# Attention gate rows by one product with ones per 512 columns, in place of columns, diagonals and a spread

## What is computed

```python
cond = jax.nn.silu(c)
mod = cond @ mod_w[i] + mod_b[i]
sh_m, sc_m, gt_m, sh_f, sc_f, gt_f = jnp.split(mod[:, None, :], 6, axis=-1)
h = rms_norm(x, norm_g[i, 0]) * (1.0 + sc_m) + sh_m
y = swa_sink_attention(h, w_qkv[j], w_o[j], swa_sinks[j], cos, sin)
x = x + gt_m * rms_norm(y, norm_g[i, 1])
h = rms_norm(x, norm_g[i, 2]) * (1.0 + sc_f) + sh_f
x = x + gt_f * rms_norm(swiglu(h, ffn_w_in[i], ffn_w_out[i]), norm_g[i, 3])
```

## Time and profile before

| | us |
|---|---|
| median of 3 runs | 1093.65 (1093.56 to 1093.86) |
| profiled execution | 1093.3 |
| its span on the engines | 1091.5 |
| PE busy | 1057.7 (97%) |
| DVE busy | 688.9 (63%) |
| ACT busy | 488.8 (45%) |
| POOL busy | 23.4 (2%) |

### The profile page before, as it was taken

One profiled execution on the slowest core, in us unless ns is written; L12 is line 12 of the kernel. 1 busy time (PEld: TensorE's weight loads), 2 busy tenths in 40 slices (PEclk: granted clock), 3 DMA queues, 4 the chain that ended last, 5 costly groups with the idle time before them and its releaser, 6 DMA issues.

```text
span 1091.5 us, 13612 instructions
## 1 busy us (share of the span) xinstructions
PE 1057.7 (97%) x4976; PEld 837.1 (77%) x4976; DVE 688.9 (63%) x877; ACT 488.8 (45%) x623; POOL 23.4 (2%) x34
## 2 busy tenths in 40 slices
PE   5899999999999999999999999999999999999998
PEld 2566676667678878888888888888888888888885
DVE  3778796787889795767667545444444544444445
ACT  4433475767466334434333333343344444444444
POOL 0000000000011000000000000000000000000000
PEclk9899999999999999999999999999999999999999
DMA  9999989999984895777678555555554555555542
GB/s 360 418 417 416 414 343 355 361 410 370 370 321 165 293 355 193 308 270 299 252 272 313 214 189 190 192 192 192 192 183 164 189 193 196 192 192 192 192 154 77
DMA packets 50599, 288.23 MB, mean 264 GB/s; under 512 B 6401, under 2 KB 6401, under 8 KB 23937
## 3 DMA queue, kind: packets, MB, share of 16 engines
q1 hardware_dynamic: 47090, 268.47, 65.2%
q0 software_dynamic: 2304, 16.78, 3.8%
q10 hardware_dynamic: 1168, 2.49, 0.7%
HBM read 285.36 MB, written 2.10 MB: 263 GB/s over the span
## 4 chain that ended last, share of the span: by engine, by line
PE 78%; DMA 10%; DVE 5%; ACT 4%; issue 2%; SPq 0%; POOL 0%; ACTq 0%; DVEq 0%
PE ps L1452 25%; PE ps L1454 24%; PE ps L1453 24%; DMA raw<-in_w_qkv 5%; DMA mraw<-in_mod_w 3%; ACT whi L428 2%; DVE wlo L848 2%; PE ps L1476 2%; DMA graw<-in_mod_h 2%; DVE mraw L859 1%; PE ps L1516 1%; PE ps L1636 1%; ACT pS L529 1%; PE ps L1727 1%; ACT pS L517 0%
## 5 line engine op out<-in xcount | busy, mean ns | idle before, releaser
L848 DVE TENSOR_TENSOR wlo<-raw,whi 128x1024 fp32r<-128x1024 f32 x334 | 394.3, 1221 | 305.2 <-ACT whi L428 305.2
L428 ACT ACTIVATE whi<-raw 128x2048 fp32r<-128x2048 f32 x167 | 320.1, 1917 | 411.0 <-PE ps L1454 377.4
L1452 PE MATMUL ps<-whi,hThi 128*128 128x512 f32 x1224 | 482.4, 394 | 10.0 <-DVE hTlo L905 7.6
L1454 PE MATMUL ps<-whi,hTlo 128*128 128x512 f32 x1224 | 477.4, 390 | 0.0
L1453 PE MATMUL ps<-wlo,hThi 128*128 128x512 f32 x1224 | 477.2, 390 | 0.0
L1452 PEld LDWEIGHTS ps<-whi,hThi 128*128 128x128 f32 x1224 | 230.3, 188 | 77.0 <-issue 20.9
L1454 PEld LDWEIGHTS ps<-whi,hTlo 128*128 128x128 f32 x1224 | 230.2, 188 | 48.5
L1453 PEld LDWEIGHTS ps<-wlo,hThi 128*128 128x128 f32 x1224 | 230.5, 188 | 46.5
L859 DVE CUSTOM_DVE_ANT_0 mraw<-mraw,cb,mbias 128x1024 f32<-128x1024 f32 x64 | 80.6, 1279 | 24.3 <-DMA mraw<-in_mod_w 24.0
L859 DVE CUSTOM_DVE_ANT_0 mraw<-mraw,cb,modT 128x1024 f32<-128x1024 f32 x64 | 83.0, 1308 | 13.3 <-DMA mraw<-in_mod_w 13.1
L1452 PE MATMUL ps<-whi,oThi 128*128 128x512 f32 x112 | 45.5, 406 | 0.3 <-DVE wlo L848 0.3
(11 more groups left out here) (192 smaller groups left out, 553.5 us busy)
## 6 DMA issues: line engine op xcount, KB each, us to landing
raw<-in_w_in SPq DMA_DIRECT2D x88, 1024.0 KB, 4.8
mraw<-in_mod_w SPq DMA_DIRECT2D x128, 512.0 KB, 7.4
raw<-in_w_out SPq DMA_DIRECT2D x44, 1024.0 KB, 4.8
raw<-in_w_qkv SPq DMA_DIRECT2D x24, 1024.0 KB, 14.6
graw<-in_mod_h SPq DMA_DIRECT2D x16, 1024.0 KB, 17.4
raw<-in_w_o SPq DMA_DIRECT2D x16, 1024.0 KB, 6.7
graw<-in_mod_h POOLq DMA_DIRECT2D x12, 1024.0 KB, 8.5
x<-in_x ACTq DMA_DIRECT2D x2, 1024.0 KB, 8.5
```

The source lines that it names most:

```text
L428: A(split_of(q, s)[0], raw[:, s], ACT.Copy).then_inc(hi_done, 1)
L848: V.tensor_tensor(low[:, k], raw[:, s, k], high[:, k].bitcast(F32), ALU.subtract).then_inc(done, 1)
L1452: mm(dst, hi, high[:, n], start=start, stop=False)
L1454: return mm(dst, lo, high[:, n], start=False, stop=stop)
```

## The change

The bias of 512 gate values is written by a small transfer into row 1 of the evacuated sums (`gate_bias`, issued by ACT), where the sums are zero. One product of a 128x128 matrix of ones with the 128x512 sums then gives all 512 gate values with their bias on all partitions at once (`gate_rows`). DVE multiplies the bank by the norm's weight, which a transfer of 1 MB, issued by POOL, has put into `grow` on all partitions beforehand, and writes `grow` (`gate_row`). `columns` for n = 4 to 7, `gate_mod`, the first `vcol`, the two attention `diagonals`, the two attention `spread`s and their `grow_evac`s are gone. The four gate sums 28 to 31 stand together; `sums_out(7)` moves ahead of `hi_of(32)`. The path of the last gate keeps its form, with other counts.

```diff
+        gacc3 = at("gacc3", 42, [P, N])
-        diag1 = at("diag1", 72, [P, 8, P])
...
+        def gate_acc(n):
+            return (gacc2[:, 0], gacc2[:, 1], gacc3[:, :], gacc2[:, 0])[n - 4]
...
 ACT        def sums_out(n):
                 act.wait_ge(g_step, GP * (n + 1))
+                if n >= 4:
+                    if n == 6:
+                        act.wait_ge(rope_c, 5)
+                    if n == 7:
+                        act.wait_ge(rows_pe, 1)
+                    A(gate_acc(n), ps[:, (6, 7, 6, 5)[n - 4]], ACT.Copy).then_inc(g_evac, 1)
+                    return
...
+            def gate_bias(n):
+                act.wait_ge(g_evac, n + 1)
+                act.dma_start(gate_acc(n)[1:2, :], gbias[n - 4:n - 3, :]).then_inc(bias_in[n - 4], 16)
...
             sums_out(4)
             evac_q(2, 1)
+            gate_bias(4)
             hi_of(21)
...
             sums_out(5)
             hi_of(24)
+            gate_bias(5)
...
             sums_out(6)
+            gate_bias(6)
...            (copy_y)
+                    if w:
+                        act.wait_ge(rows_pe, 2 + w)
...
             hi_of(31)
+            sums_out(7)
             hi_of(32)
+            gate_bias(7)
             hi_of(33)
-            sums_out(7)
...
             copy_y(1, 6)
-            grow_evac(0, 4, 0)
             hi_of(35)
...
             square_y(1)
-            grow_evac(1, 6, 0)
...
 DVE
-            def gate_mod(c):
...
+            def gate_row(n):
+                cols = slice((n - 4) * N, (n - 3) * N)
+                dve.wait_ge(rows_pe, n - 3)
+                dve.wait_ge(rows_in, 16)
+                V.tensor_tensor(grow[:, cols], ps[:, ROW_BANKS[n - 4]], grow[:, cols], ALU.mult).then_inc(rows_done, 1)
...
             mods(67, 2)
+            gate_row(4)
             lo_of(32)
             mods(69, 2)
+            gate_row(5)
             lo_of(33)
             mods(71, 2)
+            gate_row(6)
             lo_of(34)
-            gate_mod(3)
-            dve.wait_ge(oT_ready, 8)
-            dve.wait_ge(mod_added, 8)
-            V.tensor_tensor(vcol[:, :], modT[:, 2 * KT:3 * KT], gcol[:, 1], ALU.mult).then_inc(vc, 1)
+            gate_row(7)
             mods(73, 2)
...
 POOL
-            pool.wait_ge(vc, 1)
-            diagonals(diag1, 0)
-            pool.wait_ge(diag_pe, 2)
-            diagonals(diag1, 1)
+            pool.wait_ge(pv_pe, 8)
+            pool.dma_start(grow[:, :], grows).then_inc(rows_in, 16)
...
 PE
+            def gate_rows(n):
+                pe.wait_ge(bias_in[n - 4], 16)
+                if n == 4:
+                    pe.wait_ge(oT_ready, 8)
+                elif n == 6:
+                    pe.wait_ge(g_evac, 8)
+                elif n == 5:
+                    pe.wait_ge(rows_done, 1)
+                else:
+                    pe.wait_ge(rows_done, 2)
+                mm(ps[:, ROW_BANKS[n - 4]], ones[:, :], gate_acc(n), start=True, stop=True).then_inc(rows_pe, 1)
...
-            columns(4)
...
-            columns(5)
...
-            columns(6)
...
             o_block(30)
-            gate_sums(28)
-            gate_sums(29)
+            for p in range(28, 32):
+                gate_sums(p)
+            gate_rows(4)
             o_block(31)
-            gate_sums(30)
-            gate_sums(31)
+            gate_rows(5)
...
             o_block(32)
-            columns(7, 5)
+            gate_rows(6)
             o_block(33)
-            spread(diag1, 0, 4, 0)
+            gate_rows(7)
             o_block(34)
-            pe.wait_ge(half_evac, 14)
-            spread(diag1, 1, 6, 0)
             o_block(35)
...
+ROW_BANKS = (4, 4, 5, 4)
```

More of the change, by code:

```diff
@@ L61, in after, with build @@
     return q + (s + n) // 4, (s + n) % 4
-def build(nc, x, crow, cT, mod_h, pos, invf, mod_w, modbT, gT, w_qkv, w_o, sinks, w_in, w_out, out):
+def build(nc, x, crow, cT, mod_h, pos, invf, mod_w, modbT, gbias, gT, grows, w_qkv, w_o, sinks, w_in, w_out, out):
     with ExitStack() as ctx:
@@ L200, in build @@
         pv_pe, oThi_done, oT_ready = sem("pv_pe"), sem("oThi_done"), sem("oT_ready")
+        bias_in = [sem(f"bias_in{s}") for s in range(4)]
+        rows_in, rows_pe, rows_done = sem("rows_in"), sem("rows_pe"), sem("rows_done")
         vc, diag_done, diag_pe, grow_done = sem("vc"), sem("diag_done"), sem("diag_pe"), sem("grow_done")
@@ L454, in sums_out @@
                 act.wait_ge(g_step, GP * (n + 1))
+                if n >= 4:
[5 more added lines that the diff above has]
+                    return
                 if n >= 2:
                     act.wait_ge(reduced, n - 1)
-                sums = gacc if n < 4 else gacc2
-                A(sums[:, n % 2], ps[:, 6 + n % 2 if n < 7 else 5], ACT.Copy).then_inc(g_evac, 1)
+                A(gacc[:, n % 2], ps[:, 6 + n % 2], ACT.Copy).then_inc(g_evac, 1)
+            def gate_bias(n):
+                act.wait_ge(g_evac, n + 1)
+                act.dma_start(gate_acc(n)[1:2, :], gbias[n - 4:n - 3, :]).then_inc(bias_in[n - 4], 16)
             for b in range(HB):
@@ L775, in f1 @@
                         if tail and u == 1 and s in (0, 2):
-                            grow_evac(s // 2, 4, 4)
+                            grow_evac(s // 2, 4)
             def gk(i, s):
@@ L1124, in gate @@
             def gate(cols, count):
-                dve.wait_ge(grow_done, count)
+                dve.wait_ge(rows_done, count)
                 V.tensor_tensor(y[:, :, cols], y[:, :, cols],
@@ L1197, in _ @@
             dve.wait_ge(ysq, 6)
-            gate(slice(2 * N, 3 * N), 4)
+            gate(slice(2 * N, 3 * N), 3)
             V.tensor_reduce(stat[:, 12:14], ssq[:, :, 0:3], AX.X, ALU.add).then_inc(ychain, 1)
@@ L1489, in sums, with columns @@
                     last.then_inc(g_step, 1)
-            def columns(n, bank=None):
+            def columns(n):
                 pe.wait_ge(g_evac, n + 1)
-                if bank is None:
-                    bank = 6 + n % 2
-                acc = gacc if n < 4 else gacc2
                 for f in range(4):
-                    last = mm(ps[:, bank, f:f + 1], acc[:, n % 2, f * P:(f + 1) * P], ones[:, 0:1],
+                    last = mm(ps[:, 6 + n % 2, f:f + 1], gacc[:, n % 2, f * P:(f + 1) * P], ones[:, 0:1],
                               start=True, stop=True)
                 last.then_inc(reduced, 1)
+            def gate_rows(n):
[9 more added lines that the diff above has]
+                mm(ps[:, ROW_BANKS[n - 4]], ones[:, :], gate_acc(n), start=True, stop=True).then_inc(rows_pe, 1)
             def gate_sums(p):
@@ L1758, in _ @@
             o_block(37, (1,), (2, 1), tiles=(0,))
-            pe.wait_ge(grow_done, 4)
+            pe.wait_ge(rows_done, 4)
             pe.wait_ge(half_evac, 16)
@@ L1799, in f1 @@
                     if tail and s == 0:
-                        spread(diag3, 0, 4, 4)
+                        spread(diag3, 0, 4)
                     if tail and s == 2:
-                        pe.wait_ge(grow_done, 6)
-                        spread(diag3, 1, 4, 4)
+                        pe.wait_ge(grow_done, 2)
+                        spread(diag3, 1, 4)
             with pe.Fori(2, FB - 1) as i:
@@ L1914 @@
         "modbT": cols(inputs["mod_b"][0]),
+        "gbias": np.ascontiguousarray(np.asarray(inputs["mod_b"])[0][2 * D:3 * D].reshape(4, N)),
         "gT": np.ascontiguousarray(gains),
+        "grows": np.ascontiguousarray(np.broadcast_to(np.asarray(inputs["norm_g"])[0, 1], (P, D))),
         "w_qkv": blocks(w_qkv),
```

29 lines of the change are left out of this document (11 added, 18 removed).

## The result

The changed kernel takes 1095.51 us (median of 22 executions, 1093.35 to 1099.64), the kernel before, run beside it, 1093.66 us (22 executions, 1092.34 to 1094.91). The ratio is 1.0019, 95% interval 1.0013 to 1.0025. Forecast were 1093.4 us and no change: the kernel became slower by 1.9 us. The profiled execution took 1096.84 us, its span is 1095.0, 3.5 us over that of before.

A forecast was written before the change was run, and what follows sets the result against it. PE was taken as the bound, with DVE almost level at block 38, where PE's gain becomes a wait; lo_of(35) starting 0.2 us earlier reaches the end: 1093.65 - 0.2 = 1093.4 us, range 1091.0 to 1095.9.

The forecast's parts named there:

- main step: DVE waits at gate_row(7) for PE; lo_of(35) starts at 310.6, 0.2 us earlier; PE waits 2.8 us at block 38.
- Rival (a): At block 38: DVE does not hold it and PE's gain is kept, -2.7 us, 1091.0 us; chance 10%.
- its own bounds, -0.6 and -1.0: Lower bounds on the forecast time: -0.6 us for the bias issue on ACT, -1.0 us for the cover of the columns.
- inner range: Whole kernel: the forecast's own range from its bounds, 1092.0 to 1094.9 us.
- The main sum: Whole kernel: -0.2 us against the median of 1093.65, so 1093.4 us; chance 69%.
- rival (c): PE's wait of 2.8 us ahead of block 38 lowers the clock to 1.2 GHz: 1096.8 us; chance 6%.
- a clock under 1.0 after 325 us: Sign that the forecast is wrong: granted clock below full after 325 us, pointing to rival (c).
- The bias issue: ACT's queue near 193 us, ahead of hi_of(21): one DMA issue adds 0.6 us, bounds 0 and 1.3.
- PE at 283 us: PE's position at 283 us against the kernel before: +0.6 - 0.8 = -0.2 us.
- the sum has 0.8 + 1.8 + 1.7 + 1.27 - 3.4: PE after 283 us: columns(7), two spreads and an idle gap removed, four products of 3.40 us added.
- Rival (b): Late transfers on DVE's chain, deciding from a landing over 8.2 us: +1 to +2.5, 1094.6 to 1096.1 us; chance 15%.
- the 291 that would have counted: grows landing later than about 291 us would stop lo_of(32) and then PE, one for one; 284 to 288 forecast.
- Rival (d): Last gate's diagonals stay, only their counts change; nothing in the tail moves; no own case or chance.

The follow-up runs named there:

- the changed kernel's repeat: The changed kernel unchanged, run again beside the kernel before on another chip: 1094.75 us, ratio 1.0013.
- the filled kernel: Three extra products of 512 columns, results unused, on PE ahead of block 38, against the changed kernel: 1093.56 us, ratio 1.0000 to the kernel before.
- the mended one: mods(73, 2) run ahead of gate_row(7) on DVE, against the changed kernel: 1094.59 us, ratio 1.0019 to the kernel before.

## Why the prediction was wrong

**What it had right.** The chain of its main step stands in the trace. Forecast: DVE waits some 3 us at `gate_row(7)` for PE (2.94 measured), PE arrives early at block 38 and waits 2.8 us (2.90; 2.64 to 2.93 in the five other profiles with this wait), nothing is left at the first spread's place, PE's gain does not arrive. `lo_of(35)` was forecast for 310.6: 311.48 in the profile with the fall at 230 us, 309.66 in one without. And where the clock holds, the time is near the forecast one: 1092.8 to 1093.5 us in the five fastest executions of the changed kernel's repeat, before beside it 1093.18. Part of that closeness is chance. With the wait filled block 38 starts at 325.65, 1.6 us earlier than in before where 0.2 was forecast; 0.8 of that is lost near 465 us, where only that profile has a wait of PE for DVE, and 0.5 behind the last activation (both below). Rival (a), the gain kept, is refuted for this order; its size nearly came once two things behind it were mended, 2.2 us of its 2.7. A slip of addition: with its own bounds, -0.6 and -1.0, the forecast's inner range starts at 1091.8, not 1092.0.

**The step that failed.** The main sum takes the 2.8 us at block 38 only as the place where PE's gain goes; it has no term for the clock behind them, and "0.2 us reaches the end" rests on that. The clock stands only in rival (c), "It decides only if PE's wait at block 38 is longer than any wait that this trace shows to leave the clock full", and its 6%. Its condition was fulfilled by the forecast itself: 2.8 us was the main case's own number, between a row of 1.72 us with full clock and one of 4.19 us with the fall. "2.8 us of waiting is in neither row" was right, and nothing in the two rows makes 6% of it rather than one half. "PE is dense up to the wait" was no protection: before the waits that follow PE is dense too. In the profiles of all kernels here ten waits of 2.17 to 2.93 us stand behind 190 us, and in six the clock fell at the wait or within 1.5 us behind it; behind those of up to 1.6 us it never did. Length alone does not decide: the three at 230 us (2.17, 2.47, 2.69) were all followed by a fall, of the seven at block 38 (2.50 to 2.93) three were; why, no run here shows. The Trainium skill, TensorE: Matmul & The Clock Gate, section HAM oscillation, tells of a kernel whose waits for transfers between bursts of matmuls throttle the clock again each time; these runs show it for single waits of 2.2 to 2.9 us in dense work, though not each time.

The price was too high and the frequency too low. A fall behind block 38 cost 1.5 us (3.4 us at half speed, two profiles) or 2.7 us (6.8 us, one profile), where (c) took 3.4, from the longer one of the earlier trace rows, as the only size. The mean clock of the 22 executions is .9944; the kernel before has .9962 to .9964 on the three chips of the experiments (beside these 22 its clock is not on record). 0.0019 · 1093 = 2.1 us, or 1.2 falls of 1.7 us in an execution as a mean, an estimate: some have none, most have one, some more. The measured median moves by 1.9 us. The time lies inside the range of 1091.0 to 1095.9; the direction is what failed, a gain of 0.2 us against a loss of 1.9 us that is clear of the noise. Two of the prediction's own signs of being wrong came: a clock under 1.0 after 325 us, and a bias issue that cost less than 0.3 us.

**Terms with another size.** (1) The bias issue: +0.6 forecast, about +0.1 measured, since ACT's queue issues it beside the running activation. In the row the first of the two issues starts at 147.16 us, when the activation ahead of them has ended (147.14), so nothing ran beside them; the bias issue waits for the sums' activation and runs beside the next one. (2) PE at 283 us: forecast -0.2. The first sum there starts at 282.09 to 282.92 in the five profiles with the same order up to there and full clock, against 283.18 in before: -1.1 to -0.3. Term 1 given back makes -0.7, in the middle of that. In the profiled execution of the changed kernel it is 284.37, +1.2, by the gate transfer's 2.69 us of waiting and the fall behind it. (3) From there to block 36 PE wins 2.9 us where the sum has 0.8 + 1.8 + 1.7 + 1.27 - 3.4 = 2.2: the gate sums standing together, and the slow first matmul behind fewer pieces, gave some more. All of this ends in the wait at block 38. (4) Behind the last activation the changed kernel takes 0.5 us more, which no term had. It is in the profiles of all ten kernels with the change (4.2 us), and in none of the four without it (3.7). The output transfers land later there, at most 3.9 instead of 3.3 us, which fits the size; why they do was not tried. It stands in each of the ten profiles, whether the clock fell or not, so it comes beside the clock's loss. The 0.8 us near 465 us in the filled kernel is in no other profile.

**Rival (b), late transfers.** `grows` is issued at 278.94 and lands after 10.5 us, at 289.4, ahead of the 291 that would have counted. `mods` 67 and 68 paid 3.7 us for it, hidden as forecast. Piece 77 came just in time (used at 318.49 with no wait before it). It made no wait in the changed kernel's profile, but it was right behind: with DVE's order mended it took the place of the wait, 2.87 us. The prediction had the landing over 8.2 us as its point; it was 8.1 in the changed kernel and 12.7 in the mended one.

**Rival (d)** made no difference to the time, as said.

## What to carry to other kernels

Where an edit takes work from a dense PE and the forecast says that the gain turns into one wait, price the wait twice: as time, and as a stretch of half speed behind it (here behind six of ten waits of 2.2 to 2.9 us, 1.5 to 2.7 us each where it could be read). Ask at the same time for the two or three next limits behind the wait (here an order on DVE, then the place of 2 MB in a transfer queue): mending one alone gave nothing, both together turned +0.19% into -0.19%. And look at the mean clock of all executions, not only at the profiled one, before a loss is put down to work.

## What of the hardware was not expected

- Work of no use made a kernel faster: three products of 0.86 us in a wait of 2.9 us, a ratio of 1.0000 instead of 1.0013 and 1.0019, mean clock .9958 instead of .9946 and .9944.
- The clock's falls are not the same from one execution to the next: one program took 1092.2 to 1099.7 us in 12 executions. In the kernels whose profile has no wait above 1.6 us behind 190 us, fastest and slowest lay 1.6 to 4.7 us apart.
- A transfer issued by ACT took 0.50 us on its queue (the three others 0.23) and delayed the next activation by 0.13 us, since it ran beside the one before.
- 512 KB landed after 6.7 us or after 12.7 us, by whether 2 MB were issued ahead of them or behind.
